# Two-layer hybrid decoder step: output projection of the prompt tiles moved into decode's tail, the layer loop unrolled without a barrier, and another order at the start

## What is computed

```python
h = rmsnorm(x, norm_w)
z = h @ w_in                       # 1024 -> 3264: q_r k_r v_r g_r | q_lat c_raw kpe_raw | g_a
o_r = groupnorm(retention(q_r, k_r, v_r, state)) * silu(g_r)        # 4 heads of 128
c, kpe = rmsnorm(c_raw), rope(rmsnorm(kpe_raw))                     # latent 256, rotary key 64
q = rmsnorm(q_lat) @ w_qb
# prompt: causal attention, keys rmsnorm(c @ w_kb), values c @ w_vb
# decode: the same over 16 pages of 128 cached latents per sequence, plus its new tokens
o_a = attention(q, c, kpe) * silu(g_a)
x = x + concat(o_r, o_a) @ w_out   # 1024 -> 1024
```

## Time and profile before

| | us |
|---|---|
| median of three runs (lowest to highest) | 1318.73 (1316.77 to 1320.38) |
| the profiled execution | 1317.68 |
| its span, first to last instruction | 1315.9 |
| PE busy in it | 1233.2 |
| DVE busy | 726.0 |
| ACT busy | 530.6 |
| POOL busy | 444.7 |

### The profile page before, as it was taken

How to read it: one execution, slowest core, us unless ns; L and a number is a source line. 1 busy time by engine, 2 the same in 40 slices (tenths; PEclk the granted TensorE clock), 3 DMA queues, 4 the chain that set the end, 5 groups by cost and what they waited for, 6 DMA issues and landing times.

```text
span 1315.9 us, 26653 instructions
## 1 busy us (share of the span) xinstructions
PE 1233.2 (94%) x8624; PEld 1133.5 (86%) x8624; DVE 726.0 (55%) x1322; ACT 530.6 (40%) x1378; POOL 444.7 (34%) x632
## 2 busy tenths in 40 slices
PE   4999999998999999969859999999989999999698
PEld 4999995777999999958859999857789999999598
DVE  5455646655666666644244556556556666666441
ACT  4221234444555555524042121344445555555230
POOL 1024045433544455520020230454335554444200
PEclk9999999999999999989969999999999999999899
DMA  9531104004632322304523311130036232222035
GB/s 314 167 102 52 51 19 114 20 4 105 181 80 80 79 81 80 81 1 121 177 68 102 102 60 44 42 108 3 17 95 191 77 82 79 79 77 75 10 113 190
DMA packets 132780, 115.95 MB, mean 88 GB/s; under 512 B 46513, under 2 KB 127346, under 8 KB 132658
## 3 DMA queue, kind: packets, MB, share of 16 engines
q1 hardware_dynamic: 132658, 114.52, 29.3%
HBM read 103.56 MB, written 13.27 MB: 89 GB/s over the span
## 4 chain that ended last, share of the span: by engine, by line
PE 43%; issue 27%; POOL 17%; POOLq 7%; DVE 3%; ACT 2%; DVEq 1%; DMA 0%; SPq 0%; ACTq 0%
POOL krs L2174 15%; PE ps L543 7%; PE ps L544 7%; PE ps L545 7%; PE ps L637 3%; POOLq L2168 2%; POOLq L2170 2%; PE ps L551 2%; PE ps L552 2%; POOL rstat L2009 2%; PE ps L793 1%; PE ps L816 1%; PE ps L794 1%; PE ps L650 1%; POOLq L2004 1%
## 5 line engine op out<-in xcount | busy, mean ns | idle before, releaser
L1864 DVE TENSOR_REDUCE kss<-ksq 128x8 f32<-128x1024 f32 x128 | 156.0, 1219 | 195.2 <-ACT ksq L1387 195.2
L543 PE MATMUL ps<-w_hi,hT_hi 128*128 128x408 f32 (+2 forms) x704 | 243.7, 346 | 0.1
L544 PE MATMUL ps<-w_lo,hT_hi 128*128 128x408 f32 (+2 forms) x704 | 241.6, 343 | 0.0
L545 PE MATMUL ps<-w_hi,hT_lo 128*128 128x408 f32 (+2 forms) x704 | 240.5, 342 | 0.0
L1387 ACT ACTIVATE ksq<-ps 128x544 f32<-128x544 f32 x256 | 160.0, 625 | 197.9 <-PE ps L964 197.9
L964 PE MATMUL ps<-wq_hi,cT_hi 128*128 128x272 f32 x1024 | 223.7, 300 | 0.0
L2174 POOL TENSOR_TENSOR krs<-kss_t,cst 128x8 f32<-128x8 f32 x128 | 209.4, 1636 | 19.0 <-issue 2.5
L964 PE MATMUL ps<-wq_hi,cT_lo 128*128 128x272 f32 x1024 | 211.8, 288 | 0.0
L964 PE MATMUL ps<-wq_lo,cT_hi 128*128 128x272 f32 x1024 | 211.7, 288 | 0.0
L964 PEld LDWEIGHTS ps<-wq_lo,cT_hi 128*128 128x128 f32 x1024 | 160.6, 188 | 0.0
L964 PEld LDWEIGHTS ps<-wq_hi,cT_lo 128*128 128x128 f32 x1024 | 160.6, 188 | 0.0
(11 more groups left out here) (198 smaller groups left out, 2015.8 us busy)
## 6 DMA issues: line engine op xcount, KB each, us to landing
ckv<-in_cache_ckv SPq DMA_DIRECT2D x256, 128.0 KB, 2.0
raw<-in_w_in SPq DMA_DIRECT2D x68, 408.0 KB, 4.2
kp<-in_cache_kpe SPq DMA_DIRECT2D x256, 32.0 KB, 1.8
raw<-in_w_out SPq DMA_DIRECT2D x16, 340.0 KB, 4.1
S<-in_state_ret SPq DMA_DIRECT2D x8, 512.0 KB, 5.8
out<-S SPq DMA_DIRECT2D x8, 512.0 KB, 3.2
z<-out SPq DMA_DIRECT2D x2, 2048.0 KB, 8.6
wqb<-in_w_qb SPq DMA_DIRECT2D x3, 1152.0 KB, 8.4
```

Of the source, the lines that this page charges most:

```text
L543: pe.matmul(out, a_hi, b_hi, start=first, stop=False)
L544: pe.matmul(out, a_hi, b_lo, start=False, stop=False)
L545: return pe.matmul(out, a_lo, b_hi, start=False, stop=last)
L1864: dve.tensor_reduce(kss[:, hs, 2 * k:2 * k + 2, :], ksq[:, q % 2, :, c0:c0 + HW].rearrange("p j (h k) -> p j h k", h=H), AX.X, ALU.add).th ...
```

## The change

It has four parts.

1. **The beginning.** `neg_half` moves to the second place of the constants. SP loads the first 129 columns (identity and -0.5, 66 KB) behind x tile 0 and the other constants behind the x tiles. PE and POOL wait for the first part alone, DVE and POOL for the rest only before the rotary step, ACT for neither. The large memset of `z` comes after the one for which ACT waits. ACT and DVE split two chunks of weights, keep tile 0, and split the other two; the square of tile 1 follows. PE turns tile 1 before the first product. The six copies from x to the output are gone: in layer 0 the old x is read from the input.
2. **Layers without loop or barrier.** `Fori(0, DEPTH)` becomes a Python loop on every engine. Counts of semaphores run on over both layers (waits get terms such as `N_PAIR * (L + 1)`), and two of the four `stage_end` are left, after the input product and after mixing. The semaphores of the first stages are cleared by SP during decode, behind the pages of sequence 1 and ahead of the old x; `fresh` says that they are. PE turns the next layer's x tile 0 ahead of the last sample product; ACT and DVE begin the next layer's splits and norms between the last x additions. Layer 1 no longer loads weights for a layer that does not follow.
3. **Output product in decode's tail.** The prompt tiles' `y` are turned and multiplied while the last sequence's softmax runs. They use PSUM banks 1, 2, 3, 4, 6 for products and 0, 5 (0, 5, 7 for x) for turns.
4. **W_out.** Group 0 gets a place of its own (`w0_hi`, `w0_lo`) and is split in the layer's first sequence, a chunk after each of pairs 4 to 7, on ACT and DVE. Group 1 (`wout1`, in free columns of `z`) is loaded right behind group 0 and split in the tail; group 2 is loaded after `dy_ps`.

Several buffers lie in other places of SBUF for that. The core of the diff:

```diff
@@ SP: start
         load_x(0)
-        sp.dma_start(cst[:, :], const).then_inc(const_in, 16)
+        sp.dma_start(cst[:, 0:FIRST], const[:, 0:FIRST]).then_inc(ident_in, 16)
         load_norm(0)
         load_w_in(0)
         for t in range(1, TILES):
             load_x(t)
+        sp.dma_start(cst[:, FIRST:], const[:, FIRST:]).then_inc(const_in, 16)
...
-        with sp.Fori(0, DEPTH) as L:
+        for L in range(DEPTH):
...
-                return sp.snap(v + L * POOL)
+                return sp.snap(v + L * POOL) if L else v
...
-            sp.wait_ge(stage, 4 * 2)
+            sp.wait_ge(stage, 4 * (2 * L + 2))
             load_seq(1, 1, None)
-            sp.wait_ge(x_out, 16 * X_OUTS)
-            sp.sem_clear(x_out)
-            sp.dma_start(z[:, 0:S_TILE, 0:D], yp_t).then_inc(xold_in, 16)
+            for s in layer_sems:
+                if s not in running_sems:
+                    sp.sem_clear(s)
+            sp.sem_inc(fresh, 1)
+            if L:
+                sp.wait_ge(x_out, 16 * X_OUTS)
+            old_p = yp_t if L else x_prompt[0].rearrange("(t p) d -> p t d", p=P)
+            sp.dma_start(z[:, 0:S_TILE, 0:D], old_p).then_inc(xold_in, 16)
...
             for k in range(4):
-                sp.dma_start(wout0[:, k, :, :], layer(w_out_t)[:, 2 * k:2 * k + 2, 0:N0]).then_inc(wout0_in, 16)
+                sp.dma_start(wout0[:, k, :, :], w_out_t[L][:, 2 * k:2 * k + 2, 0:N0]).then_inc(wout0_in, 16)
+            for k in range(4):
+                sp.dma_start(wout1[:, k, :, :], w_out_t[L][:, 2 * k:2 * k + 2, OG[1]:OG[2]]).then_inc(wout1_in, 16)
...
+            sp.wait_ge(dy_ps, L + 1)
+            for k in range(4):
+                sp.dma_start(raw[:, k, :, 0:n], w_out_t[L][:, 2 * k:2 * k + 2, OG[2]:OG[3]]).then_inc(raw_in[k], 16)
...
+            if L + 1 < DEPTH:
+                sp.wait_ge(out_ps, N_OUT * L + NTH[0, S_TILE])
+                load_norm(L + 1)
+                load_small(L + 1)
+                store(0)
+                for k in range(4):
+                    sp.wait_ge(w_lo_ok, N_W * L + 4 * (NG + 2) + k + 1)
+                    sp.dma_start(raw[:, k, :, :], w_in_t[L + 1][:, 2 * k:2 * k + 2, 0:GW]).then_inc(raw_in[k], 16)
+            store(1)
+            store(2)
@@ PE: y_turn(0) stands ahead of the last pair's keys; behind the last sequence
+            y_turn(1)
+            out_product(0, 0)
+            y_turn(2)
+            out_begin(0, 1)
+            tail_max_turn(last)
+            out_end(0, 1)
+            tail_max_spread(last)
+            y_turn(3)
+            out_begin(0, 2)
+            tail_attend(last, 1)
+            out_end(0, 2)
+            tail_den(last)
+            out_begin(0, 3)
+            tail_turn(last)
+            out_end(0, 3)
+            decoded_values()
+            out_begin(1, 0)
+            y_turn(S_TILE)
+            out_end(1, 0)
+            out_product(0, S_TILE)
+            for t in range(1, TILES):
+                out_product(1, t)
+            for t in range(S_TILE):
+                out_product(2, t)
+            if L + 1 < DEPTH:
+                pe.wait_ge(fresh, L + 1)
+                x_turn(0)
+            out_product(2, S_TILE)
@@ ACT
+            def split_out(g, chunks=range(4)):
+                for k in chunks:
+                    if k == 0 and g == 0:
+                        act.wait_ge(wout0_in, 16 * 4 * (L + 1))
...
             def sequence(seq, b, first, last):
...
                     square_pair(n, seq, b, q, first and q < 2)
                     if q == 3 and not first:
                         tail_exp(seq - 1, 1 - b)
+                    if first and q >= 4:
+                        split_out(0, (q - 4,))
@@ DVE, in a sequence: between the low copy of pair q + 1 and the sum of pair q
+                    if first and q >= 4:
+                        split_out(0, (q - 4,))
+                    if last and q + 1 == PAIRS:
+                        keep_y_lo(0)
                     sum_pair(n, b, q)
@@ DVE, behind the last sequence
+            keep_y_lo(1)
+            half_scores(last, 1, 1)
+            tail_max(last, 1)
+            keep_y_lo(2)
+            tail_diag(last)
+            tail_shift(last, 1)
+            keep_y_lo(3)
+            tail_den(last, 1)
+            split_out(1)
+            dve.wait_ge(xold_in, 32 * (L + 1))
+            x_add(0, 0, L)
+            x_add(0, 1, L)
+            tail_divide(last)
+            x_add(0, 2, L)
+            tail_keep(last)
+            x_add(0, 3, L)
+            decoded_y()
+            keep_y_lo(S_TILE)
+            x_add(1, 0, L)
+            x_add(0, S_TILE, L)
+            x_add(1, 1, L)
+            split_out(2)
```

More of the change, by code:

```diff
@@ L545, in product, with tile_products @@
             return pe.matmul(out, a_lo, b_hi, start=False, stop=last)
-        def tile_products(out, t, w_h, w_l):
-            for c in range(DC):
+        def tile_products(out, t, w_h, w_l, chunks=range(DC), w0=None):
+            for c in chunks:
+                if w0 is not None and c % 2 == 0:
+                    pe.wait_ge(w_lo_ok, w0 + c // 2 + 1)
                 if t == S_TILE:
@@ L579, in _, with x_turn, tile_product @@
-        pe.wait_ge(const_in, 16)
-        with pe.Fori(0, DEPTH) as L:
-            def tile_product(g, par, t, first):
-                if first:
+        pe.wait_ge(ident_in, 16)
+        for L in range(DEPTH):
+            def x_turn(t):
+                n = rows(t)
+                pe.wait_ge(x_normed, t + 1)
+                for half in range(2):
+                    u = 2 * t + half
+                    if u >= 3:
+                        pe.wait_ge(x_lo, u - 2)
+                    for c in range(4):
+                        m = pe.transpose(ps[:, X_BANKS[u % 3], c * P:c * P + n], zc(t, H0 + (4 * half + c) * P, P),
+                                         ident[0:n, 0:n])
+                    m.then_inc(x_turned, 1)
+            def tile_product(g, t):
+                if g == 0:
@@ L610, in latents @@
+            if L == 0:
+                x_turn(0)
+            x_turn(1)
+            for t in range(TILES):
+                if t >= 1 and t + 1 < TILES:
+                    x_turn(t + 1)
+                tile_product(0, t)
+            for g in range(1, NG):
+                pe.wait_ge(w_lo_ok, N_W * L + g * 4 + 4)
+                for t in range(TILES):
+                    tile_product(g, t)
+            stage_end(pe, L, 0)
             def latents(t):
@@ L1449, in _ @@
+                sequence(i * 2 + S1, 0, False, False)
+            last = S1 + NB - 1
+            sequence(last, 1, False, True)
+            keep_y_hi(1)
+            keep_y_hi(2)
+            split_out(1)
+            tail_exp(last, 1)
+            keep_y_hi(3)
+            keep_y_hi(S_TILE)
+            move_out(0, L)
             split_out(2)
-            for g in range(3):
-                move_out(g)
-            layer_end(act, "scalar")
+            move_out(1, L)
+            if L + 1 == DEPTH:
+                move_out(2, L)
@@ L1474, in _ @@
         dve.sem_inc(cleared, 2)
-        dve.wait_ge(const_in, 16)
-        with dve.Fori(0, DEPTH) as L:
-            dve.wait_ge(norm_in, 16)
+        dve.memset(z[ST:P, S_TILE, :], 0.0)
+        for L in range(DEPTH):
             def norm(t):
```

692 lines of the change are left out of this document (367 added, 325 removed).

## The result

| | us |
|---|---|
| before, median (lowest to highest) | 1318.11 (1316.77 to 1320.38) |
| after, median (lowest to highest) | 1332.88 (1329.90 to 1333.44) |
| ratio after to before | 1.0106, 95% interval 1.0085 to 1.0127 |
| after, the profiled execution and its span | 1333.15, span 1331.2 |

The change makes the kernel 1.1% slower, which is little but clear of noise; between the two profiled spans, 1315.86 and 1331.25 us unrounded, lie 15.4 us. From the page of the changed kernel: its first lines, two lines of the 40 slices (tenths; PEclk is the granted clock) and the chain that ended last, by engine.

The account below looks back on a forecast made before the run. The prediction took the matrix engine as the bound almost everywhere. From 1317.7 us it subtracted gains of 3.6, 41.6 and 19.8 and added 77.0 of stalls, giving 1329.7, stated as 1330 us, range 1317 to 1343.

Parts of the forecast that it names:

- part 1: Kernel's beginning: with fewer constants loaded in front, the first product starts at 17.5, 3.6 us gained.
- part 2: Layer 0's tail into layer 1: matrix work back to back gains 40.5 us, faster clock 1.1 more, 41.6 in all.
- part 3: Layer 1's tail: shortened from 82.0 to 62.2 us, 19.8 gained.
- part 4: First sequence: ScalarE waits for W_out's group 0, delaying pair 7's turn 36.0 us; 38.5 lost per layer, 77.0 in all.
- every us there counts twice: W_out's landing in the first sequence: any error in its predicted time is paid in both layers.
- the walk: Tail: VectorE's new order set against the matrix engine's work, 63.8 us in sum; all answers but one came in time.
- The wait for the late denominator: Tail: VectorE divides after four split chunks and two x additions, making the matrix engine wait about 1.2 us.
- The cover of 14 us: Between layers: layer 1's first w_in group lands about 622 and is needed at 636.
- Rival D: Between layers: first w_in group lands over 14 us later than thought, the old 13.3 us return; 1343, chance 0.04.
- everything behind arrives 875 / 408 x 1.08 = 2.3 us earlier: Beginning: only 66 KB of constants stay in front, so later loads gain 2.3 us at the weights' rate.
- Rival A: First sequence: W_out's load is there when ScalarE asks at pair 4, so no stall; 1257 us, chance 0.09.
- Rival C: Tail keeps its handshakes behind VectorE, 13 us idle a layer, otherwise as forecast; 1356 us, chance 0.04.

Follow-up runs that it names:

- p1_tail_together: a3_early_load with the tail's interleaving undone: softmax steps and decoded values together, then all group 0 products; VectorE divides before adding to x; 1289.5 us.
- c1_act_issue: Changed kernel with W_out's group 0 issued by ScalarE behind pair 3's work in the first sequence, instead of by SP behind the page loads; 1272.5 us.
- a2_late_split: Changed kernel with W_out's group 0 split in a layer's last sequence (pairs 0, 2, 3, 5) instead of its first; loads unmoved; 1263.4 us.
- b3_x_behind_split_ahead: a3_early_load with the old x and W_out's second group issued behind all pages, VectorE's split still ahead of the page sum; 1260.2 us.
- a1_clears_behind: Changed kernel with SP's 76 semaphore clears behind both groups of W_out instead of ahead of them; 1324.7 us.
- a3_early_load: Changed kernel with W_out's group 0 issued by SP ahead of sequence 1's pages instead of behind them, the clears and the old x; 1261.0 us.
- d2_w0_before_x: Changed kernel with W_out's group 0 issued behind the clears but ahead of the old x instead of behind it; 1321.1 us.
- b2_x_behind_pages: b1_split_behind_sum with the old x and W_out's second group issued behind all pages instead of ahead of sequence 2's; 1256.9 us.
- s1_const_front: Changed kernel with the 877 KB of later constants loaded right behind the identity again, ahead of the norm weight and first weights; 1333.7 us.
- b1_split_behind_sum: a3_early_load with VectorE's part of the W_out split behind the page sum in pairs 5 to 7, instead of ahead in pairs 4 to 7; 1260.9 us.
- q1_w_in_later: b2_x_behind_pages with layer 1's first w_in group issued behind the store of output group 1 instead of ahead of it; 1257.3 us.

## Why the prediction was right, and where it was not

The sum came out at 1329.7 for a measured 1332.9. Its terms stand here against the marks of the two traces. In the changed kernel the matrix engine turns the first tile of y ahead of the last pair, which lengthens the last sequence by 0.8 us; so the measured terms of parts 2 and 3 count from the start of the last sequence.

| term | predicted | measured |
|---|---|---|
| part 1, first product (until decode starts) | 3.6 | 2.1 (2.7) |
| part 2, tail to layer 1's first product | 40.5 | 39.9 |
| part 2, clock behind it | 1.1 | 1.05 |
| part 3 | 19.8 | 19.2 |
| part 4, both layers | 77.0 | 78.3 |
| change of the span | +12.0 | +15.4 |

All four parts miss in the same direction, by 0.6 to 1.3 us each (part 1 counted until decode starts).

**Part 4** was right in kind and size: the wait stands where it was put, and ScalarE's idle time of 34.52 us, the empty stretch from 329.75 to 365.71 and the clock of 0.50 in it are what the prediction named. From decode's start to the turn of pair 7 pass 24.62 us before and 60.73 after, 36.1 late for 36.0. Under the sum two errors cancel. Against the first page load the issue comes 1.8 us later than before (its first page load stands at 291.80 instead of 294.14): the clears took 4.2 of the 4.6 expected, and page numbers without the layer's term gave back 2.4, not 4.0. So the issue is 1.2 later than predicted. But I had let the last load take the longest landing of the earlier trace rows, 11.2; it was issued near 351.1 and took 10.1. That the turn came out within 0.1 us is this luck. What follows the turn in layer 0 (low clock, the other three chunks) costs 3.2 us instead of 2.5. The doubling ("every us there counts twice") was measured directly: 3.8 us of landing moved the time by 8.2.

**Part 2 and part 3** hold within 0.7 us a layer, but three terms of the walk were mis-sized and partly cancel. From the last sequence's start to layer 1's first product the changed kernel needs 0.6 us more than the sum allows:

- The products take 54.0 us, 0.161 per matmul, not 52.7. I had taken 0.157 from groups 1 and 2 of the kernel before, where products stand back to back; broken up by turns and steps of the tail they take a little longer.
- The wait for the late denominator, 1.2 us, never came. From the last pair to the next layer's first product the matrix engine works 63.75 of 63.78 us.
- The decoded values I let take half of their 1.96 us, as if these had run at half clock; in the changed kernel they take 1.96 too:

```profile
631.37 1.96 PE L1107 MATMUL ps<-wvb,olat 128*64 128x128 f32 x16
```

This last error was in reading the clock of a neighbouring stretch for theirs. A window of just these 2 us in the kernel before gives 1.00, 2 us behind ten at 0.50:

```profile
577.00:587.00 10.00, 5.69 (x38) 0.50 0.00 1
...
589.21:591.20 1.99, 1.96 (x16) 1.00 0.00 0
```

In p1_tail_together the same matmuls fall into a stretch of lower clock in layer 0 and take 2.95 us, 3.67 in layer 1. The interleaving's own share, not separated in the prediction, is 14.3 us a layer.

**The cover of 14 us** of layer 1's first group was wrong, though it cost nothing. I set the landing against the first product, and put it 50 us behind the last pair, where the last load landed at 53.8. But behind the landing stand ScalarE's four chunks, then the square, the root and the norm of tile 0, and the matrix engine turns that tile first. In the changed kernel:

```profile
663.45 0.89 ACT L1186 ACTIVATE w_hi<-raw 128x816 fp32r<-128x816 f32 x1 [0.20 <-DMA raw<-in_w_in]
664.24 1.05 ACT L1169 ACTIVATE z<-z 128x1024 f32<-128x1024 f32 x1
...
666.49 1.28 DVE L1588 SCALAR_TENSOR_TENSOR z<-z,rstat,norm_b 128x1024 f32<-128x1024 f32 x1 [0.69 <-POOL rstat L2166]
...
669.28 1.03 PE L593 MATMUL ps<-cst,z 128*128 128x128 f32 x8
```

The norm ends at 667.77 and is asked for at 669.28: 1.5 us. Rival D needed a landing not 14 but some 2 us late. Its chance of 0.04 was too small.

**Part 1** failed in one step: "everything behind arrives 875 / 408 x 1.08 = 2.3 us earlier". I priced bytes at the rate of a queue that runs full. In this part of the kernel they cost 1.03 us, as undone alone; why so little is not shown. The step after it, the square of tile 1 at 12.3, fell with it (13.78). The steps behind that hold: 3.6 us from the square to the transposes (3.5 predicted) and 1.6 on to the first product (1.7).

**Rival A** (the load in time, 1257) was worked out well as a time: the kernels in which the load is in time take 1261.0, and 1256.9 with the next limits gone. What decided against it was the length of SP's queue, and c1_act_issue shows that this reason was the true one. The rule of the Trainium skill that stood behind it spoke for a landing near 321; the rows spoke against it, and they were right. **Rival C** gave 13 us a layer for a tail with its handshakes; with the interleaving taken back it costs 14.3, of which 9.1 to 9.8 are idle and the rest the clock.

## What to carry to other kernels

When work is moved forward, the data it needs must be followed back through the queue of the engine that issues the load: here a split moved forward by some 260 us met a load that landed 34 us too late for it, though 230 us early for its old place. Order the issuing queue by who needs what first; one block moved in SP's queue turned +1.1% into -4.3%, and two more moves into -4.8%. When a fix gives nothing, compare the traces stretch by stretch before dropping it: two limits may stand one behind the other, and then only both fixes pay.

## What the runs showed of the hardware that was not expected

- The time from issue to landing is not the load's. The same 344 KB loads took 9.8 us in the median behind 2.3 MB, 4.1 to 4.4 with the queue clear, and 5.1 issued by ScalarE.
- Decode's first pairs run at 1.2 GHz in some profiled executions and not in others, though the matrix engine did the same before (idle 0.69 twice, 0.73 and 1.36 us). It costs 1.5 us per layer: from decode's first matmul to the first rotary product pass 5.75 or 7.29 us. It was so in both layers of a2_late_split, b3_x_behind_split_ahead and p1_tail_together, in layer 1 alone in a1_clears_behind, a3_early_load, c1_act_issue, d2_w0_before_x, b2_x_behind_pages and s1_const_front, and in neither in the kernel before, the changed kernel, b1_split_behind_sum and q1_w_in_later. No edit explains it, and b1_split_behind_sum, c1_act_issue and p1_tail_together, one of each kind, ran on the same chip; the cause stays open. The stretch in the changed kernel and in a2_late_split:

```profile
304.00:308.00 4.00, 1.91 (x16) 1.00 0.18 45
308.00:312.00 4.00, 4.00 (x35) 1.00 0.45 123
```

```profile
304.00:308.00 4.00, 1.91 (x15) 1.00 0.21 54
308.00:312.00 4.00, 4.00 (x22) 0.57 0.45 115
```

- Four DMA issues cost ScalarE 3.1 us in layer 0, 1.47 of it for the first, and 2.0 in layer 1, some 0.5 each; on SP the four took 1.9 to 2.2.
